# Scattering each expert's rows of a mixture-of-experts layer in two half-row transfers on separate chains

## The chip, the core and the metric

The kernel runs on one NeuronCore of a Trainium2 chip. The metric is the device time of one execution in microseconds (us). TensorE (PE, with its weight loads as PEld), VectorE (DVE), ScalarE (ACT), GpSimd (POOL) and SyncE (SP) each run their own instruction stream in order; they meet through semaphores, and 16 DMA engines move data between HBM and the on-chip memories.

## The reference, cut to what matters

```python
# x1 = x + token mixers (512 tokens, 1024 columns)
h2 = rmsnorm(x1, g_ffn)
scores = sigmoid(h2 @ w_router); top 8 of 64 experts per token -> gates (512 x 64)
for e in range(64):
    hmid = silu(h2 @ w_gate_e[e]) * (h2 @ w_up_e[e]) * gates[:, e]     # 256 wide
    routed += hmid @ w_down_e[e]                                       # 1024 wide
out = x1 + shared_swiglu(h2) + routed
```

512 tokens choose 8 experts each, so an expert has 64 tokens on average.

## The kernel before, in words

The token mixers and the router come first and take about 470 us. Then follows the expert stage, one step for each of the 64 experts, with tokens gathered 96 slots at a time (a set of 128 partition rows; the unused ones hold the index 1024 or more and are dropped by the bounds check).

For expert k a step has these parts. **SP** loads 3 MB of weights into one of four slots (`load_w`, L502). **ACT** and DVE split each weight into a high part (ACT, `gu_hi_k` L969 and `split_wd` L916) and a low part (DVE, `gu_lo_k` L1446 and `low_wd` L1457), because every product is computed as three. Both DVE lines subtract one SBUF tensor from another. **PE** makes gate and up (L1834), turns the gathered rows of the next expert (L1862), makes the down product of the expert before (L1848) in two halves of 512 columns, turns the middle (L1842) and finds the slots of a later expert (L1855). **ACT** copies each half of the down product from PSUM into `y` (`copy_y`, L934), one of two buffers. DVE works out the row indices `idxg` (L1414, four buffers), and ACT keeps a copy, `idxs` (`keep_idx`, L983), since a gather's index buffer is overwritten before the scatter is done with it.

**POOL** issues both indirect transfers. `gather` (L609) fetches the rows of expert k+5 from `hn_dram`. `scatter` (L615) adds the rows of `y` into `out` in HBM, by accumulating DMA. Before each of them POOL runs `take_turn` (L605), a tiny addition of 16 elements that reads and writes SBUF and has its own semaphore. In `scatter_k` POOL waits for both halves of `y`, for the kept indices, and for the scatter before to have landed, as two scatters may add to the same row of `out`. Around expert k the order on POOL is written out by hand:

```python
def pair(k, u):
    scatter_k(k, u, 5 + 2 * k)
    gather_k(k + 5, (u + 1) % 4, 6 + 2 * k)
```

It runs for experts 0 to 58; the last five experts have a scatter alone. Two other waits hang on a scatter's landing: ACT's `y_i` before it writes a `y` buffer again (two experts later), and `keep_idx` before it writes an index buffer again (four experts later). At the end POOL waits for the last scatter; a loop for experts with over 96 tokens follows and is entered only if there are any.

Of the kernel before, what the change touches and what calls it, by code (L numbers as in the profile page):

```python
# [31 lines left out]
P = 128  # L32
# [18 lines left out]
def layer(nc, x, g_mix, w_in, q_norm_a, k_norm_a, q_norm_b, k_norm_b, rel_bias, b_forget, w_gate, b_gate,  # L51
# [4 lines left out]
    E, D, F = w_gate_e.shape  # L56
    N = x.shape[1]
# [6 lines left out]
    COLS = 512  # L64
# [3 lines left out]
    SH = NT  # L68
# [81 lines left out]
    with ctx:  # L150
        def sb(name, shape, dt=f32):
            return ctx.enter_context(nc.sbuf_tensor(name, shape, dt))

        def sem(name):
            return ctx.enter_context(nc.semaphore(name))
# [18 lines left out]
        gsum = sb("gsum", [P, NT]); ginv = sb("ginv", [P, NT]); m8 = sb("m8", [P, NT, 8])  # L174
        gate = sb("gate", [P, 4])
        idxg = [sb(f"idxg{i}", [P, 1], u32) for i in range(4)]
        idxs = [sb(f"idxs{i}", [P, 1], u32) for i in range(4)]
        hn_ss, hn_ms, hn_r = sb("hn_ss", [P, NT]), sb("hn_ms", [P, NT]), sb("hn_r", [P, NT])
        rbias = sb("rbias", [P, E])

# [143 lines left out]
        wd_hi_ready, wd_ready, o_wd_hi, o_wd, o_midT_hi = sem("wd_hi_ready"), sem("wd_ready"), sem("o_wd_hi"), sem("o_wd"), sem("o_midT_hi")  # L324
        y_psum, y_ready = sem("y_psum"), sem("y_ready")
        based = [sem(f"based{i}") for i in range(2)]
        scattered, pool_set, turns = sem("scattered"), sem("pool_set"), sem("turns")
        o_free, o_pos, o_onehot, o_idx_psum, o_idx, o_gathered = (
            sem("o_free"), sem("o_pos"), sem("o_onehot"), sem("o_idx_psum"), sem("o_idx"), sem("o_gathered"))
        o_xT_psum, o_xT, o_gu, o_silu, o_mid, o_midT_psum, o_midT, o_y_psum, o_y, o_scattered = (  # L330
# [14 lines left out]
        def after(eng, s, n):  # L345

            if not isinstance(n, int) or n > 0:
                eng.wait_ge(s, n)
# [223 lines left out]
        def _(pool):  # L572
# [24 lines left out]
            for i in range(4):  # L597
                nc.gpsimd.memset(xg[i], 0.0).then_inc(pool_set, 1)
            pool.wait_ge(pool_set, 5)
            last_row = pool.to_reg(N - 1)  # L600

            def take_turn(before):

# [9 lines left out]
            def scatter(slot, idx, before, done):  # L613
                take_turn(before)
                pool.indirect_dma_start(out=out_rows, out_offset=bass.IndirectOffsetOnAxis(idx[:, 0:1], 0),  # L615
                                        in_=y[slot], in_offset=None, bounds_check=last_row, oob_is_err=False,
                                        compute_op=ALU.add).then_inc(done, 16)

            def gather_k(k, slot, before):
                after(pool, xT_psum, k - 3)  # L620
                pool.wait_ge(idx_ready, k + 1)
                gather(slot, before, gathered[slot])

            def scatter_k(k, u, before):
                pool.wait_ge(y_ready, 2 * (SH + k + 1))
                pool.wait_ge(idx_kept, k + 1)
                after(pool, scattered, 16 * k)
                scatter(u % 2, idxs[u], before, scattered)

            for k in range(5):  # L630
                gather_k(k, k % 4, k)
# [1 line left out]
                pool.wait_ge(b, 8 * SH)  # L633

            def pair(k, u):
                scatter_k(k, u, 5 + 2 * k)
                gather_k(k + 5, (u + 1) % 4, 6 + 2 * k)

            for k in range(4):
                pair(k, k)  # L640
# [4 lines left out]
                pair(k, k % 4)  # L645
            more = pool.value_load(rounds_i[0:1, 0:1], min_val=0, max_val=ROUNDS - 1)
            for k in range(E - 5, E):
                scatter_k(k, k % 4, 5 + 2 * (E - 5) + k - (E - 5))
            pool.wait_ge(scattered, 16 * E)

            with pool.If(more > 0):
                with pool.Fori(0, more * E) as it:
                    pool.wait_ge(o_idx, it + 1)
                    gather(0, 2 * E + 2 * it, o_gathered)
                    pool.wait_ge(o_y, it + 1)
                    scatter(0, idxg[0], 2 * E + 2 * it + 1, o_scattered)
                    pool.wait_ge(o_scattered, 16 * it + 16)
            with pool.Else():
                pass
# [2 lines left out]
        def _(act):  # L662
# [278 lines left out]
            def y_i(it, n):  # L941
                if isinstance(it, int) and it == SH:
                    for b in based:
                        act.wait_ge(b, 8 * SH)
                after(act, scattered, 16 * (it - SH - 1))
                for h in range(2):
                    act.wait_ge(y_psum, 2 * it + h + 1)
                    copy_y(n, h).then_inc(y_ready, 1)

# [29 lines left out]

            def keep_idx(k, u):  # L980
                act.wait_ge(idx_ready, k + 1)
                after(act, scattered, 16 * (k - 3))
                nc.scalar.activation(idxs[u][:], idxg[u][:], ACT.Copy).then_inc(idx_kept, 1)  # L983

            def step(it, n, slot, more=True):
                k = it - SH
# [611 lines left out]
        def _(pe):  # L1598
# [356 lines left out]

            more = pe.value_load(rounds_i[0:1, 0:1], min_val=0, max_val=ROUNDS - 1)
            with pe.If(more > 0):
                pe.wait_ge(scattered, 16 * E)
                with pe.Fori(0, more * E) as it:
                    nc.tensor.matmul(psM[0:1, 0:1], ident_b[:, 0:1], ident_b[:, 0:1], start=True, stop=True).then_inc(o_free, 1)  # L1960
                    pe.wait_ge(o_onehot, it + 1)
                    find_slots(0, it % E).then_inc(o_idx_psum, 1)
                    pe.wait_ge(o_gathered, 16 * it + 16)
                    transpose_rows(0).then_inc(o_xT_psum, 1)
                    pe.wait_ge(o_xT, it + 1)
                    for k in range(2):
                        pe.wait_ge(w_in_sem[0][k], 8 * E + 32 * it + 32)
                    gate_up(0, P, xT_all, 0).then_inc(o_gu, 1)
                    pe.wait_ge(o_mid, it + 1)
                    transpose_mid(0, P).then_inc(o_midT_psum, 1)  # L1970
                    pe.wait_ge(o_midT, it + 1)
                    pe.wait_ge(o_wd, it + 1)
                    down(0, 0, P)
                    down(0, 1, P).then_inc(o_y_psum, 1)
                    pe.wait_ge(o_y, it + 1)
# [55 lines left out]
```

## Time and profile before

| | us |
|---|---|
| median of 3 runs (lowest to highest) | 1109.51 (1108.78 to 1111.87) |
| the profiled execution, its time | 1109.88 |
| its span in the trace | 1107.9 |
| PE busy | 1082.7 (98%) |
| DVE busy | 882.5 (80%) |
| ACT busy | 738.8 (67%) |
| POOL busy | 317.4 (29%) |

All times in the rows below are microseconds from the start of the span. In a row of a timeline stand the start, the duration, the engine, the line of the kernel, the operation, output<-input with their shapes, and in square brackets how long the engine was idle before it and what ended that. Where a row stands for several instructions (x2), its duration runs from the first's start to the last's end. DVE instructions overlap by some 0.08 us at their ends. A page of the profile gives the busy time of each engine as a share of the whole span, so the expert stage has to be read by windows.

### The profile page before, as it was taken

Reading aid. Unit: us, or ns where it says so; the run is one execution under the profiler, and the core shown is the slowest. Engines: PE = TensorE matmul, PEld = TensorE weight load, DVE = VectorE, ACT = ScalarE, POOL = GpSimd, SP = SyncE. Lnnn points to the kernel's source line nnn. Section 1 sums busy time; section 2 is a strip of 40 time slices with the busy share of each in tenths; the row PEclk is TensorE's granted clock in tenths of the full one; section 3 lists DMA queues with packets and bytes.
Section 4 is the critical chain, followed back from the end, with each engine's and each line's share of the span. In section 5 each row is a group of like instructions: output and inputs, shape, how many; then the busy total and the mean of one; then the engine's idle time right before and its main releaser. Section 6 shows DMA issues by size and latency. Waiting matters only on the chain.

```text
span 1107.9 us, 19464 instructions
## 1 busy us (share of the span) xinstructions
PE 1082.7 (98%) x5809; PEld 893.6 (81%) x5809; DVE 882.5 (80%) x1405; ACT 738.8 (67%) x1304; POOL 317.4 (29%) x293
## 2 busy tenths in 40 slices
PE   8999999999999999999999999999999999999994
PEld 7789978777777887678888888888888888888883
DVE  6644376478865845579999999999999999999993
ACT  5434464444346521168888888888888888888883
POOL 1221022000000001137444444444444444434332
PEclk9999999999999999999999999999999999999998
DMA  7233212421532093669999999999999999999972
GB/s 248 78 108 106 92 41 75 152 76 39 134 114 96 7 381 138 245 231 366 382 388 384 385 376 377 376 384 386 383 375 385 377 380 377 381 380 382 378 273 36
DMA packets 97353, 284.71 MB, mean 257 GB/s; under 512 B 19683, under 2 KB 22251, under 8 KB 96924
## 3 DMA queue, kind: packets, MB, share of 16 engines
q1 hardware_dynamic: 78876, 250.52, 59.4%
q0 software_dynamic: 18432, 33.61, 12.2%
q8 instruction: 26, 0.43, 0.1%
q14 instruction: 19, 0.16, 0.0%
HBM read 279.79 MB, written 37.81 MB: 287 GB/s over the span
## 4 chain that ended last, share of the span: by engine, by line
PE 61%; DMA 24%; DVE 8%; issue 3%; ACT 2%; POOL 2%; POOLq 0%; SPq 0%; ACTq 0%; DVEq 0%
DMA out<-arena,idxs 23%; PE bank L1660 21%; PE bank L1834 17%; PE bank L1848 8%; PE bank L1808 3%; PE bank L1862 3%; PE bank L1604 2%; PE bank L1822 2%; DVE w_lo L1095 1%; POOL turn L605 1%; ACT arena L795 1%; DMA arena<-in_w_in 1%; PE bank L1842 1%; DVE gu_parts L1446 1%; PE bank L1716 1%
## 5 line engine op out<-in xcount | busy, mean ns | idle before, releaser
L1834 PE MATMUL bank<-gu_parts,xT_parts 128*128 128x512 f32 x1280 | 338.9, 394 | 0.9 <-DVE gu_parts L1446 0.5
L1834 PEld LDWEIGHTS bank<-gu_parts,xT_parts 128*128 128x128 f32 x1280 | 235.3, 188 | 47.6 <-DVE gu_parts L1446 0.9
L1848 PE MATMUL bank<-w_lo 128*128 128x512 f32 x804 | 201.6, 399 | 0.0
L605 POOL TENSOR_TENSOR turn<-minus_half 16x1 f32<-16x1 f32 x128 | 101.2, 791 | 349.5 <-DMA out<-arena,idxs 307.3
L1848 PEld LDWEIGHTS bank<-w_lo 128*128 128x128 f32 x804 | 146.3, 188 | 28.5 <-issue 0.5
L615 POOL DMA_INDIRECT out<-arena,idxs x64 | 123.4, 1927 | 19.4 <-issue 10.2
L1660 PE MATMUL bank<-w_hi,hT_hi 128*128 128x512 f32 (+1 forms) x320 | 124.4, 389 | 0.4 <-DVE w_lo L1095 0.4
L1660 PE MATMUL bank<-w_hi,hT_lo 128*128 128x512 f32 (+1 forms) x320 | 121.7, 380 | 0.0
L1660 PE MATMUL bank<-w_lo,hT_hi 128*128 128x512 f32 (+1 forms) x320 | 121.4, 380 | 0.0
L1446 DVE TENSOR_TENSOR gu_parts<-arena_x,gu_parts 128x1024 fp32r<-128x1024 f32 x96 | 116.8, 1216 | 2.4 <-ACT gu_parts L969 2.2
L1446 DVE TENSOR_TENSOR gu_parts<-arena,gu_parts 128x1024 fp32r<-128x1024 f32 x96 | 116.8, 1216 | 2.4 <-ACT gu_parts L969 2.3
L1095 DVE TENSOR_TENSOR w_lo<-arena,w_hi 128x512 fp32r<-128x512 f32 (+1 forms) x112 | 69.2, 667 | 47.3 <-ACT w_hi L694 47.3
L969 ACT ACTIVATE gu_parts<-arena_x 128x1024 fp32r<-128x1024 f32 x96 | 101.5, 1057 | 7.4 <-PE bank L1834 3.4
L969 ACT ACTIVATE gu_parts<-arena 128x1024 fp32r<-128x1024 f32 x96 | 101.5, 1057 | 5.9 <-DMA arena<-in_w_up_e 4.1
L934 ACT ACTIVATE arena<-bank 128x512 f32<-128x512 f32 x128 | 76.7, 600 | 29.3 <-PE bank L1848 27.3
L1834 PE MATMUL bank<-gu_more,xT_parts 128*128 128x512 f32 x256 | 89.3, 389 | 0.0
L609 POOL DMA_INDIRECT arena<-hn_dram,idxg x64 | 82.1, 1283 | 12.0 <-issue 6.6
L694 ACT ACTIVATE w_hi<-arena 128x512 fp32r<-128x512 f32 (+1 forms) x112 | 61.4, 605 | 29.5 <-PE bank L1660 17.1
L579 POOL TENSOR_TENSOR hn_r<-hn_ms,minus_half 128x1 f32<-128x1 f32 x8 | 4.4, 556 | 251.5 <-DVE hn_ms L1071 251.5
L1457 DVE TENSOR_TENSOR w_lo<-arena,w_lo 128x1024 fp32r<-128x1024 f32 x64 | 75.3, 1218 | 0.3 <-ACT w_lo L916 0.3
L1457 DVE TENSOR_TENSOR w_lo<-arena_x,w_lo 128x1024 fp32r<-128x1024 f32 x64 | 75.3, 1217 | 0.2 <-ACT w_lo L916 0.2
L579 POOL TENSOR_TENSOR rnorm<-mean,minus_half 128x8 f32<-128x8 f32 x20 | 32.8, 1638 | 144.7 <-DVE mean L1170 144.7
(226 smaller groups left out, 1988.6 us busy)
## 6 DMA issues: line engine op xcount, KB each, us to landing
arena<-in_w_gate_e SPq DMA_DIRECT2D x64, 512.0 KB
arena<-in_w_up_e SPq DMA_DIRECT2D x64, 512.0 KB
arena<-in_w_down_e SPq DMA_DIRECT2D x64, 512.0 KB
arena_x<-in_w_gate_e SPq DMA_DIRECT2D x64, 512.0 KB
arena_x<-in_w_up_e SPq DMA_DIRECT2D x64, 512.0 KB
arena_x<-in_w_down_e SPq DMA_DIRECT2D x64, 512.0 KB
arena<-in_w_in SPq DMA_DIRECT2D x14, 1024.0 KB, 5.5
arena<-in_w_gate SPq DMA_DIRECT2D x8, 1024.0 KB, 5.8
```

The lines of the kernel that those rows point to most:

```text
L605: nc.gpsimd.tensor_tensor(turn[:], minus_half[0:16, 0:1], minus_half[0:16, 0:1], ALU.add).then_inc(turns, 1)
L609: pool.indirect_dma_start(out=xg[slot], out_offset=None, in_=hn_dram, in_offset=bass.IndirectOffsetOnAxis(idxg[slot][:, 0:1], 0), bounds_c ...
L615: pool.indirect_dma_start(out=out_rows, out_offset=bass.IndirectOffsetOnAxis(idx[:, 0:1], 0), in_=y[slot], in_offset=None, bounds_check=la ...
L694: nc.scalar.activation(split_of(w_hi, c, j), raw_of(c, j), ACT.Copy).then_inc(split_hi, 1)
L934: return nc.scalar.activation(y[n][:, h * 512:(h + 1) * 512], psY[h][:], ACT.Copy)
L969: nc.scalar.activation(gu_hi[c].rearrange("p g j c -> p g (j c)"), wgu[slot][:, :, PER * c:PER * (c + 1), :].rearrange("p g j c -> p g (j ...
L1095: nc.vector.tensor_tensor(split_of(w_lo, c, j), raw_of(c, j), split_of(w_hi, c, j).bitcast(f32), ALU.subtract).then_inc(split_lo, 1)
L1446: nc.vector.tensor_tensor(flat(gu_lo[c]), flat(raw_part), flat(gu_hi[c]).bitcast(f32), ALU.subtract).then_inc(gu_lo_ready, 1)
L1457: return nc.vector.tensor_tensor(low[:, :, cols], wd[slot][:, :, cols], high[:, :, cols].bitcast(f32), ALU.subtract)
L1660: last = nc.tensor.matmul(psD[n % 2][:, 0:chunk_cols(c)], left, right, start=(j == 0 and k == 0), stop=(j == ND - 1 and k == 2))
L1834: last = nc.tensor.matmul(out_, a[:, PER * c + j, :], b[c][:, :, j, :], start=(c == 0 and j == 0 and i == 0), stop=(c == CHUNKS - 1 and j ...
L1848: last = nc.tensor.matmul(psY[h][0:rows, :], midT[n][a][:, j, 0:rows], w[b][:, j, h * 512:(h + 1) * 512], start=(j == 0 and k == 0), stop= ...
```

## The change

The index tile of a scatter gets two columns. ACT writes 2i and 2i+1 into them instead of i, and `out` is seen as 1024 half rows of 512 columns. An expert's scatter becomes two, one for each half of the columns of `y`, each with its own semaphore. Each half waits for its own half of `y` and for the same half of the expert before; ACT's copy of a half waits for that half alone. Each has its own turn. All 128 index rows are walked in each of the two.

```diff
-        idxs = [sb(f"idxs{i}", [P, 1], u32) for i in range(4)]
+        idxs = [sb(f"idxs{i}", [P, 2], u32) for i in range(4)]
...
-        scattered, pool_set, turns = sem("scattered"), sem("pool_set"), sem("turns")
+        scattered, pool_set, turns = [sem(f"scattered{h}") for h in range(2)], sem("pool_set"), sem("turns")
...
+            def scatter_half(h, slot, idx, before):
+                take_turn(before)
+                pool.indirect_dma_start(out=out_halves, out_offset=bass.IndirectOffsetOnAxis(idx[:, h:h + 1], 0),
+                                        in_=y[slot][:, h * COLS:(h + 1) * COLS], in_offset=None, bounds_check=last_half, oob_is_err=False,
+                                        compute_op=ALU.add).then_inc(scattered[h], 16)
...
             def scatter_k(k, u, before):
-                pool.wait_ge(y_ready, 2 * (SH + k + 1))
                 pool.wait_ge(idx_kept, k + 1)
-                after(pool, scattered, 16 * k)
-                scatter(u % 2, idxs[u], before, scattered)
+                for h in range(2):
+                    pool.wait_ge(y_ready, 2 * (SH + k) + h + 1)
+                    after(pool, scattered[h], 16 * k)
+                    scatter_half(h, u % 2, idxs[u], before + h)
...
             def pair(k, u):
-                scatter_k(k, u, 5 + 2 * k)
-                gather_k(k + 5, (u + 1) % 4, 6 + 2 * k)
+                scatter_k(k, u, 5 + 3 * k)
+                gather_k(k + 5, (u + 1) % 4, 7 + 3 * k)
...
-                after(act, scattered, 16 * (it - SH - 1))
                 for h in range(2):
+                    after(act, scattered[h], 16 * (it - SH - 1))
                     act.wait_ge(y_psum, 2 * it + h + 1)
                     copy_y(n, h).then_inc(y_ready, 1)
...
                 act.wait_ge(idx_ready, k + 1)
-                after(act, scattered, 16 * (k - 3))
-                nc.scalar.activation(idxs[u][:], idxg[u][:], ACT.Copy).then_inc(idx_kept, 1)
+                for done in scattered:
+                    after(act, done, 16 * (k - 3))
+                nc.scalar.activation(idxs[u][:, 0:1], idxg[u][:], ACT.Copy, scale=2.0)
+                nc.scalar.activation(idxs[u][:, 1:2], idxg[u][:], ACT.Copy, scale=2.0, bias=1.0).then_inc(idx_kept, 1)
```

## Rows read from the trace of the kernel before

**Rows 1.** Busy time by windows: stretch, its length, then busy us of PE, PEld, DVE, ACT, POOL, granted clock, DMA share, GB/s

```profile
600.00:700.00 100.00, 100.00 (x526) 84.64 (x525) 97.40 (x137) 87.25 (x137) 43.87 (x43) 1.00 1.03 380
...
1000.00:1050.00 50.00, 49.86 (x260) 42.01 (x260) 47.90 (x67) 43.10 (x67) 20.21 (x20) 1.00 1.03 378
```

**Rows 2.** Timeline of PE: the row transposes of two experts in succession

```profile
725.42 1.05 PE L1862 MATMUL bank<-cst,arena 128*128 128x128 f32 x8
...
734.94 1.05 PE L1862 MATMUL bank<-cst,arena 128*128 128x128 f32 x8
```

**Rows 3.** Waits over the whole span: who waited for what, us in total, times, longest

```profile
POOL turn L605 <- DMA out<-arena,idxs: 249.2, 51, 6.1
ACT xT_parts L978 <- PE bank L1862: 23.4, 50, 0.5
```

**Rows 4.** Timeline of POOL over one expert in mid-stage

```profile
726.50 0.98 POOL L605 TENSOR_TENSOR turn<-minus_half 16x1 f32<-16x1 f32 x1 [4.89 <-DMA out<-arena,idxs]
727.63 1.59 POOL L615 DMA_INDIRECT out<-arena,idxs  x1 [0.16 <-issue]
728.72 1.22 POOL L605 TENSOR_TENSOR turn<-minus_half 16x1 f32<-16x1 f32 x1
730.08 1.05 POOL L609 DMA_INDIRECT arena<-hn_dram,idxg  x1
735.97 1.02 POOL L605 TENSOR_TENSOR turn<-minus_half 16x1 f32<-16x1 f32 x1 [4.85 <-DMA out<-arena,idxs]
```

**Rows 5.** Timeline of DVE in the same stretch

```profile
721.67 2.35 DVE L1457 TENSOR_TENSOR w_lo<-arena,w_lo 128x1024 fp32r<-128x1024 f32 x2
...
726.21 1.22 DVE L1446 TENSOR_TENSOR gu_parts<-arena_x,gu_parts 128x1024 fp32r<-128x1024 f32 x1
...
728.67 1.21 DVE L1446 TENSOR_TENSOR gu_parts<-arena_x,gu_parts 128x1024 fp32r<-128x1024 f32 x1
...
731.19 1.22 DVE L1457 TENSOR_TENSOR w_lo<-arena_x,w_lo 128x1024 fp32r<-128x1024 f32 x1
```

**Rows 6.** Timeline of POOL where the expert stage begins

```profile
493.60 6.05 POOL L605 TENSOR_TENSOR turn<-minus_half 16x1 f32<-16x1 f32 x1 [5.77 <-issue]
...
502.26 1.62 POOL L615 DMA_INDIRECT out<-arena,idxs  x1 [0.16 <-POOL turn L605]
503.35 5.49 POOL L605 TENSOR_TENSOR turn<-minus_half 16x1 f32<-16x1 f32 x1
508.99 1.06 POOL L609 DMA_INDIRECT arena<-hn_dram,idxg  x1
...
512.07 7.39 POOL L615 DMA_INDIRECT out<-arena,idxs  x1 [0.52 <-DVE gate L1415]
```

**Rows 7.** Timeline of DVE beside the turn at 503.35

```profile
503.04 2.35 DVE L1457 TENSOR_TENSOR w_lo<-arena_x,w_lo 128x1024 fp32r<-128x1024 f32 x2
...
507.58 1.21 DVE L1446 TENSOR_TENSOR gu_parts<-arena,gu_parts 128x1024 fp32r<-128x1024 f32 x1
```

**Rows 8.** Timeline of POOL and DVE around 754 us

```profile
753.65 1.22 DVE L1446 TENSOR_TENSOR gu_parts<-arena_x,gu_more 128x1024 fp32r<-128x1024 f32 x1
754.28 0.63 POOL L605 TENSOR_TENSOR turn<-minus_half 16x1 f32<-16x1 f32 x1 [4.44 <-DMA out<-arena,idxs]
```

**Rows 9.** DMA queues: packets, MB, share of 16 engines, in 732.5 to 733.5, then in 728 to 732

```profile
q0 software_dynamic: 35, 0.14, 71.5%
...
q1 hardware_dynamic: 458, 1.67, 102.3%
```

**Rows 10.** Timeline of ACT: the kept indices, and the split that follows

```profile
722.35 0.20 ACT L983 ACTIVATE idxs<-idxg 128x1 uint32<-128x1 uint32 x1
722.44 1.06 ACT L969 ACTIVATE gu_parts<-arena_x 128x1024 fp32r<-128x1024 f32 x1
```

**Rows 11.** Timeline of the end: the last copy of y, the last two scatters

```profile
1094.17 1.56 POOL L615 DMA_INDIRECT out<-arena,idxs  x1 [0.46 <-issue]
1095.11 0.60 ACT L934 ACTIVATE arena<-bank 128x512 f32<-128x512 f32 x1 [0.72 <-PE bank L1848]
...
1099.62 1.56 POOL L615 DMA_INDIRECT out<-arena,idxs  x1 [0.46 <-issue]
```

**Rows 12.** Chain that ended last: start, us; the landing of the last scatter but one

```profile
1094.17 4.57 DMA out<-arena,idxs
```

More of the change, by code:

```diff
@@ L599, in _ @@
             pool.wait_ge(pool_set, 5)
-            last_row = pool.to_reg(N - 1)
+            last_row, last_half = pool.to_reg(N - 1), pool.to_reg(2 * N - 1)
+            out_halves = out_rows.rearrange("t (h c) -> (t h) c", h=2)
             def take_turn(before):
@@ L647, in _ @@
             for k in range(E - 5, E):
-                scatter_k(k, k % 4, 5 + 2 * (E - 5) + k - (E - 5))
-            pool.wait_ge(scattered, 16 * E)
+                scatter_k(k, k % 4, 5 + 3 * (E - 5) + 2 * (k - (E - 5)))
+            for h in range(2):
+                pool.wait_ge(scattered[h], 16 * E)
             with pool.If(more > 0):
@@ L653, in _ @@
                     pool.wait_ge(o_idx, it + 1)
-                    gather(0, 2 * E + 2 * it, o_gathered)
+                    gather(0, 3 * E + 2 * it, o_gathered)
                     pool.wait_ge(o_y, it + 1)
-                    scatter(0, idxg[0], 2 * E + 2 * it + 1, o_scattered)
+                    scatter(0, idxg[0], 3 * E + 2 * it + 1, o_scattered)
                     pool.wait_ge(o_scattered, 16 * it + 16)
@@ L1957, in _ @@
             with pe.If(more > 0):
-                pe.wait_ge(scattered, 16 * E)
+                for done in scattered:
+                    pe.wait_ge(done, 16 * E)
                 with pe.Fori(0, more * E) as it:
```

## The prediction

> **What bounds the kernel now.** I read the busy time by windows first, since the page's shares mix stages. In the expert stage PE is busy 100.00 of 100 us, DVE 97.4, ACT 87.3, POOL only 43.9, and the DMA engines are full (share 1.03, 380 GB/s) [rows 1]. PE turns rows every 9.52 us (725.42 to 734.94), so an expert costs 9.52 us and PE sets it [rows 2]. In 1000 to 1050 PE is still busy 49.86 of 50. Next come the waits: POOL's turn waits 249 us in all for scatters to land, 51 times [rows 3]. That looks like slack on POOL, and like a chain the change would loosen. Neither holds without a look at when POOL can work, so the third view is POOL's timeline beside DVE's.
>
> There a pattern shows. DVE's splits (L1446, L1457) read two SBUF tensors. POOL's turn takes 0.98 us at 726.50 and ends 0.05 after the split that ends at 727.43; the next takes 1.22 us, at 728.72, and ends 0.06 after the one that ends at 729.88 [rows 4, 5]. An addition of 16 elements needs no such time: it is shut out. So POOL works in two windows per expert: 727.43 to 728.67 (1.24 us), where scatter is issued, and 729.88 to 731.19 (1.31), where gather is. From 731.19 on five splits follow without a gap, two of L1457 and three of L1446 (the same five stand from 721.67 to 727.43: 5.76 us) [rows 5]. One job, turn and issue, uses 727.43 to 728.72, 1.29 us, in the first window, and 729.88 to 731.13, 1.25, in the second [rows 4]. Both windows are full: 2.54 of 2.55 us. The 4.9 us that POOL waits for landings lie inside the closed block, where it couldn't have worked in any case.
>
> That a job which comes too late pays for the whole block can be read where the stage begins: a turn of 6.05 us at 493.60, one of 5.49 at 503.35, an issue of 7.39 at 512.07 [rows 6]. The turn at 503.35 began just as L1457 did (503.04) and ended at 508.84, 0.05 behind the last L1446 (507.58 + 1.21) [rows 7].
>
> **The change, part by part.**
>
> *POOL's third job.* Each of experts 0 to 58 now has three jobs (two halves and a gather), each with its turn, in place of two. All 128 index rows are walked in each, so I price a half's job like a whole one's, 1.25 us of open time. The low bound is half of that by bytes: then three jobs need 2.5 us, fit, and the term is 0; but the walk is over rows, and gather, a plain transfer of the same 128 rows, takes as long as scatter does. Three jobs need 3.75 us of open time and DVE's pattern has 2.55. Since gathers and scatters must keep pace with experts, DVE has to stand still until the rest fits: 3.75 - 2.55 = 1.20 us per expert at least. How it comes to stand: POOL falls behind, ACT's copy of y (a buffer written again two experts later) waits for a half to land, the middle's copy and the down split queue behind that copy on ACT, and DVE has nothing to do between its single split and the next L1457. POOL's second window opens wider there. PE then waits for the down split and the middle. The upper bound: the opening comes when a landing is late, not when POOL asks; a turn that just misses pays one more split of 1.21 us, so 2.41. Farther out, a third job that always pays for the whole block gives three windows per expert, one and a half DVE patterns: 14.28 us, 4.76 more. I take 1.60: the 1.20, and 0.4 for turns that miss, since a turn falls into a split at any point and then waits half of it, 0.6 us, and two of three jobs can meet one (2/3 x 0.6 = 0.4). Experts that pay: 59, less 2 that the second y buffer and the gathers ahead cover: 57. Term: 57 x 1.60 = +91 us; bounds 57 x 1.20 = +68 and 57 x 2.41 = +137.
>
> *ACT's second index copy.* An index copy takes ACT from 722.35 to 722.44, 0.09 us until the next starts [rows 10]; once more per expert. Hidden: ACT waits 0.5 us for the row transposes in each of 50 experts [rows 3]. Without that cover, 64 x 0.09 = 6 us. Taken as 0. ACT's and keep_idx's further waits for a second semaphore cost nothing where the first is waited for already.
>
> *The packets.* Bytes stay. In the stretch with only accumulating packets on the software queue 35 of them hold 71.5% of 16 engines for 1 us: 0.327 us each; a plain one costs 1.023 x 4 x 16 / 458 = 0.143 [rows 9]. A half row's packet may cost 0.164 (by bytes) or 0.327 (by packet). The added DMA time per expert lies between 0 and 64 x 0.327 / 16 = 1.3 us. As the cost of a whole one is 2.3 times a plain one's, as two passes over the bytes would give, I take it by bytes, near 0. In my case even 1.3 would be hidden: a step of 11.1 us leaves the engines 1.6 more.
>
> *The waits between halves.* Behind POOL's wait for the first half's landing stand the second half and the gather. A scatter was issued at 727.63 and had landed by 735.97 [rows 4]; with its two chains each half has a whole step for that, so these waits end before the windows open, as now. Priced 0.
>
> *The end.* The last five experts have two jobs, as before, so no stretch. The last scatter is issued at 1099.62 although y was ready at 1095.71; it waited for the one before, 4.57 us from issue to landing [rows 11, 12]. After: the first half of expert 62 at 1092.4, the second 2.2 later, landing in 3.9 to 4.57, then the last half by 1099.1 to 1099.9, landed at 1103.0 to 1104.5, where now it is 1099.62 + 4.57 = 1104.2. Term: -1 us (-1.2 to +0.3).
>
> Sum against the profiled execution's own time: 1109.9 + 91 - 1 = 1200 us (its span is 1107.9, 2.0 less; its time lies 0.4 above the median of 1109.51, too little to correct).
>
> A rule is to be weighed against this. POOL's turn at 503.35 met four borders between splits and was let in at none of them [rows 6, 7]; the one at 754.28 was let in at the first border, 754.91 (753.65 + 1.22 is 754.87) [rows 8]. The Trainium skill (SBUF — State Buffer, section on the two separate sides) says that DVE with two SBUF inputs and a GpSimd operation that reads SBUF exclude each other, whoever is first, for the whole instruction. By that rule as it stands each border would let POOL in, and the third job would pay some 1.2 us of waiting inside a block of 5.76 and nothing on the path. The row at 503.35 speaks against it, that at 754.28 for it. Without the rule the case stands as a rival:
>
> **The rivals.**
>
> *POOL gets in between splits.* If turns like that at 754.28 are the rule, three jobs, each 1.25 plus at most 1.22 of waiting, fit in 9.52 (7.4 us). Then the body stays at 9.52 us per expert, and the packets go by bytes. The end gives its -1: 1109 us, 1107 to 1113. For it: the turn at 754.28. Against: that was a turn, while the issue at 512.07 stayed shut out for 7.39 us [rows 6], and one job per window is all that POOL does.
>
> *The body holds and the end is shorter*, the faster case. If POOL has room, scatters may also follow their data more closely; the last half would be issued as soon as the last y is there, 1095.71 + 0.6, and land 4.57 later: 1100.9 in place of 1104.2, 3.3 less, and up to 1 more if a half lands sooner. 1105.5 us. It decides from the point where the second half of expert 62 lands before 1096, which needs its issue by 1091.5, a us ahead of its data: hard.
>
> *DMA becomes the bound.* POOL has room, but an accumulating half packet costs what a whole one does: 1.3 us per expert over 58 experts is +75, and -1 at the end: 1184 us. For it: the engines are full, and nothing shows a shorter accumulating packet. Against: plain packets here go by bytes.
>
> *The whole block each time*: 57 x 4.76 = +271: 1381 us.
>
> **How the numbers follow.** Forecast 0.66; POOL gets in 0.13; shorter end 0.08; DMA 0.09; whole block 0.04. A measurement of this kernel can tell about 0.3% (3.3 us) from no change. Faster: 0.08. Same: 0.11 of the 0.13. Slower: 0.66 + 0.09 + 0.04 + 0.02 = 0.81. The likeliest case's own range is 1177 to 1246; openings that come still later, as far as one more split for a second job (57 x 0.6 = 34 on average), draw it up to 1280, and a lighter half job down to the case of no change. To hold 8 in 10 the low end must reach into the case of no change: 1108 to 1280.
>
> **What would show it.** Right: PE transposes 10.7 to 12 us apart in mid-stage, often in two alternating lengths; turns or issues on POOL of 5 to 7 us beside unbroken splits in each step or each second; ACT's copy of y waiting for the scatter's DMA; the DMA share under 1. Wrong: steps of 9.52, with turns of about 1 us inside the block (then POOL gets in), or a DMA share of 1 with ACT waiting for weights (then the packets). A half's issue well under 1 us would break the first term.

## The result, and the profile after

The changed kernel takes 1117.3 us (median of 4 runs, 1114.12 to 1119.11) where the kernel before, on the same chip, takes 1109.17: a ratio of 1.0071, 95% interval 1.0056 to 1.0086. It is slower, by 0.7%. The profiled execution took 1117.17 us, its span is 1115.4. Of the 83 us that the forecast stood too high, nearly all lies in one term.

Busy time by windows of the changed kernel, in the columns of [rows 1], shows where the time isn't and where it is:

```profile
600.00:700.00 100.00, 100.00 (x526) 84.63 (x525) 97.41 (x136) 88.20 (x146) 78.07 (x63) 1.00 1.04 381
900.00:1000.00 100.00, 98.88 (x506) 82.29 (x505) 92.89 (x131) 83.31 (x142) 74.53 (x63) 1.00 1.04 375
```

In mid-stage PE is as busy as in [rows 1]; POOL's share has gone from 43.87 to 78.07 us of 100 and nobody waits for it. From 900 on PE has gaps; the count of its matmuls shows more than the busy time does, 506 in 100 us where it was 526. The row transposes of PE (its timeline, [rows 2]) date the loss. The changed kernel:

```profile
906.98 1.05 PE L1873 MATMUL bank<-cst,arena 128*128 128x128 f32 x8
916.77 1.05 PE L1873 MATMUL bank<-cst,arena 128*128 128x128 f32 x8
...
946.56 1.05 PE L1873 MATMUL bank<-cst,arena 128*128 128x128 f32 x8
956.80 1.05 PE L1873 MATMUL bank<-cst,arena 128*128 128x128 f32 x8
...
1085.30 1.05 PE L1873 MATMUL bank<-cst,arena 128*128 128x128 f32 x8
```

The kernel before:

```profile
1011.41 1.05 PE L1862 MATMUL bank<-cst,arena 128*128 128x128 f32 x8
1021.25 1.05 PE L1862 MATMUL bank<-cst,arena 128*128 128x128 f32 x8
...
1078.37 1.05 PE L1862 MATMUL bank<-cst,arena 128*128 128x128 f32 x8
```

From 506 to 906.98 the steps are 9.52 to 9.57 us in both, as in [rows 2], and the two kernels are some 0.4 us apart. Then the changed kernel's become 9.79, later 10.24 at 956.80, and the last transposes come 6.93 us later than before (1085.30 against 1078.37). The kernel before has the same break, later and milder, at 1021.25 (9.84). What PE misses there is named by the waits between 900 and 1080 us (who waited for what, us in total, times, longest); the changed kernel:

```profile
DVE gu_parts L1457 <- ACT gu_parts L978: 12.9, 18, 1.4
...
ACT gu_parts L978 <- DMA arena<-in_w_up_e: 10.4, 8, 1.8
ACT gu_parts L978 <- DMA arena_x<-in_w_up_e: 9.1, 6, 2.0
```

In the kernel before the first of the two DMA rows reads (the second: 2.1 us, 3 times, 0.8):

```profile
ACT gu_parts L969 <- DMA arena<-in_w_up_e: 4.1, 5, 1.1
```

Weights come late. The DMA queues say why (packets, MB, share of 16 engines, 600 to 900 us). Before:

```profile
q1 hardware_dynamic: 26640, 97.00, 81.2%
q0 software_dynamic: 9178, 17.08, 22.0%
```

After:

```profile
q1 hardware_dynamic: 26545, 96.66, 80.7%
q0 software_dynamic: 13762, 17.14, 23.8%
```

The software queue (gathers and scatters) moves the same bytes in half as many packets again and takes 1.8% of 300 us more: 5.4 us of all 16 engines over 31.5 experts, 0.17 us per expert. Where no short packets mix in, one accumulated packet of the software queue takes 0.327 us for a whole row [rows 9] and 0.176 for a half (66.0% of 16 engines for 0.5 us, over 30 packets; changed kernel, 725.5 to 726):

```profile
q0 software_dynamic: 30, 0.06, 66.0%
```

Two halves so cost 8% more than one whole. The lead of the loads can be read at SP, which issues them: it waits until DVE has read the slot that the next load will overwrite, and as long as it waits, the loads are ahead. SP's waits from 800 to 900 us, kernel before, then changed kernel:

```profile
SPq L502 <- DVE w_lo L1457: 25.8, 10, 4.9
```

```profile
SPq L502 <- DVE w_lo L1468: 8.9, 6, 3.2
```

(SPq is SP's queue; the columns are those of the waits above.) From 700 to 800 they are 61.0 and 48.4 us, from 900 to 1000 they are 0.8 and nothing. How long the lead lasts also differs between runs: tail_halves, below, which is the kernel before up to the last expert, still has 32.1 us from 900 to 1000. In these two profiles the lead is gone earlier in the changed kernel, and its steps break some eleven experts earlier. From there each step lasts as long as its transfers take: 9.93 us on average from 906.98 to 1055.93, where PE would need 9.53. That is more than the added 0.17, since the whole excess shows once the lead is gone; the kernel before has 9.65 in its few late steps (1011.41 to 1059.68).

What the prediction thought impossible stands in POOL's timeline of the changed kernel (start, duration; compare [rows 4]):

```profile
601.76 0.98 POOL L606 TENSOR_TENSOR turn<-minus_half 16x1 f32<-16x1 f32 x1 [1.53 <-DMA out<-arena,idxs]
602.90 2.39 POOL L622 DMA_INDIRECT out<-arena,idxs  x1 [0.16 <-issue]
604.76 0.60 POOL L606 TENSOR_TENSOR turn<-minus_half 16x1 f32<-16x1 f32 x1
605.60 2.13 POOL L622 DMA_INDIRECT out<-arena,idxs  x1 [0.24 <-issue]
607.19 0.60 POOL L606 TENSOR_TENSOR turn<-minus_half 16x1 f32<-16x1 f32 x1
608.03 1.73 POOL L610 DMA_INDIRECT arena<-hn_dram,idxg  x1 [0.24 <-issue]
611.19 1.08 POOL L606 TENSOR_TENSOR turn<-minus_half 16x1 f32<-16x1 f32 x1 [1.44 <-DMA out<-arena,idxs]
```

Beside it the splits in DVE's timeline, same kernel:

```profile
602.61 1.21 DVE L1457 TENSOR_TENSOR gu_parts<-arena_x,gu_parts 128x1024 fp32r<-128x1024 f32 x1
...
607.60 2.35 DVE L1468 TENSOR_TENSOR w_lo<-arena,w_lo 128x1024 fp32r<-128x1024 f32 x2
609.87 1.22 DVE L1457 TENSOR_TENSOR gu_parts<-arena_x,gu_parts 128x1024 fp32r<-128x1024 f32 x1
611.01 1.22 DVE L1457 TENSOR_TENSOR gu_parts<-arena_x,gu_more 128x1024 fp32r<-128x1024 f32 x1
```

The five-split block begins at 607.60, and gather is issued at 608.03, inside it. The first scatter's issue at 602.90 lies beside the split at 602.61 too. Issues are not shut out there; they only last longer, 1.73 to 2.39 us where they take 1.05 to 1.59 in [rows 4]. (One issue on record stands against this, the 7.39 us in [rows 6]; more_bytes and before_less, below, have it at the same place, 7.42 and 7.39 us, and the kernels with three jobs don't. It stays unexplained.) The turn at 611.19 begins inside the block and is let in at the border at 612.23 (611.01 + 1.22), with the block's last split still to come. From the first turn to the end of gather's issue three jobs take 8.0 us (601.76 to 609.76) of 9.53.

The kernel before had shown the same already. One hundred us ahead of the expert in [rows 4] its POOL and its DVE read:

```profile
631.51 2.06 POOL L615 DMA_INDIRECT out<-arena,idxs  x1 [0.50 <-PE bank L1862]
633.87 1.60 POOL L609 DMA_INDIRECT arena<-hn_dram,idxg  x1 [0.24 <-issue]
```

```profile
633.34 1.22 DVE L1446 TENSOR_TENSOR gu_parts<-arena,gu_parts 128x1024 fp32r<-128x1024 f32 x1
```

Gather's issue begins inside a split. Of the 42 scatters issued from 600 to 1000 us 23 last 1.6 us as in [rows 4] and 19 last 2.0 to 2.4. Even in [rows 4] the issue at 727.63 runs to 729.22, past the split's start at 728.67 [rows 5].

At the end of the span, the timelines of ACT and POOL in the changed kernel, to be set beside [rows 11]:

```profile
1101.86 0.60 ACT L943 ACTIVATE arena<-bank 128x512 f32<-128x512 f32 x1 [0.78 <-PE bank L1859]
1103.66 0.18 POOL L606 TENSOR_TENSOR turn<-minus_half 16x1 f32<-16x1 f32 x1 [0.38 <-DMA out<-arena,idxs]
1104.31 1.56 POOL L622 DMA_INDIRECT out<-arena,idxs  x1 [0.47 <-POOL turn L606]
...
1106.83 1.56 POOL L622 DMA_INDIRECT out<-arena,idxs  x1 [0.90 <-issue]
```

From the end of the last copy of y (1102.46) to the end of the span are 12.9 us; before, 1107.9 - 1095.71 = 12.2. The end costs 0.7 us more; with the 6.93 of the steps (some 0.4 of it from before the stage's steps) that is the difference of the spans, 7.5, within 0.2.

### The profile page after: what moved, and what is told of

Same layout as the page of the kernel before. It is cut to its first block, busy times and chain, and to the rows that moved or that the text cites. A ratio compares the mean times of both kernels' runs of the same rounds, so it can differ in the third digit from the quotient of the medians.

```text
span 1115.4 us, 19794 instructions
## 1 busy us (share of the span) xinstructions
PE 1087.5 (98%) x5809; PEld 895.1 (80%) x5809; DVE 882.0 (79%) x1405; ACT 742.0 (67%) x1368; POOL 497.7 (45%) x421
## 4 chain that ended last, share of the span: by engine, by line
PE 76%; DVE 8%; SPq 7%; DMA 3%; ACT 2%; issue 2%; POOL 1%; ACTq 0%; DVEq 0%; POOLq 0%
PE bank L1845 26%; PE bank L1671 21%; PE bank L1859 13%; SPq L502 7%; PE bank L1873 4%; PE bank L1819 3%; PE bank L1615 3%; PE bank L1833 2%; DMA arena<-in_w_up_e 2%; DVE w_lo L1106 1%; PE bank L1853 1%; DVE gu_parts L1457 1%; ACT arena L804 1%; PE bank L1727 1%; PE bank L1740 1%
## 5 line engine op out<-in xcount | busy, mean ns | idle before, releaser
L622 POOL DMA_INDIRECT out<-arena,idxs x128 | 262.6, 2051 | 31.5 <-issue 26.0
L606 POOL TENSOR_TENSOR turn<-minus_half 16x1 f32<-16x1 f32 x192 | 161.0, 839 | 163.1 <-DMA out<-arena,idxs 88.8
L978 ACT ACTIVATE gu_parts<-arena 128x1024 fp32r<-128x1024 f32 x96 | 101.4, 1057 | 11.3 <-DMA arena<-in_w_up_e 10.4
L610 POOL DMA_INDIRECT arena<-hn_dram,idxg x64 | 94.3, 1473 | 12.9 <-issue 11.8
```

Of the source, the lines that this page charges most:

```text
L606: nc.gpsimd.tensor_tensor(turn[:], minus_half[0:16, 0:1], minus_half[0:16, 0:1], ALU.add).then_inc(turns, 1)
L610: pool.indirect_dma_start(out=xg[slot], out_offset=None, in_=hn_dram, in_offset=bass.IndirectOffsetOnAxis(idxg[slot][:, 0:1], 0), bounds_c ...
L622: pool.indirect_dma_start(out=out_halves, out_offset=bass.IndirectOffsetOnAxis(idx[:, h:h + 1], 0), in_=y[slot][:, h * COLS:(h + 1) * COLS ...
L978: nc.scalar.activation(gu_hi[c].rearrange("p g j c -> p g (j c)"), wgu[slot][:, :, PER * c:PER * (c + 1), :].rearrange("p g j c -> p g (j ...
```

## The experiments

Three theories were to be told apart: that POOL's room between DVE's splits is the price (the forecast, theory P), that it is time on the full DMA engines (theory D), and that the two chains matter in themselves.

**DMA engines with room.** The kernel before and the changed one, each with the same part of the loads of w_down_e left out from expert 8 on (three quarters of the columns of the second half of the rows, 0.39 MB per expert):

```diff
-                    sp.dma_start(dst[:, i * rows:(i + 1) * rows], src[:, i * rows:(i + 1) * rows]).then_inc(w_in_sem[n][k], 16)
+                    cols = D // 4 if short and i else D if k == 2 else F
+                    sp.dma_start(dst[:, i * rows:(i + 1) * rows, 0:cols], src[:, i * rows:(i + 1) * rows, 0:cols]).then_inc(w_in_sem[n][k], 16)
...
-                    load_w(n, 2, k)
+                    load_w(n, 2, k, short=True)
```

> The kernel before, with the second half of w_down_e loaded for 256 of its 1024 columns from expert 8 on, so 0.39 MB less per expert (the down weights used are then partly stale). Theory D (DMA engines full: half packets cost more engine time, weights come late in the last third): the kernel before loses only about 1 us to late weights (steps of 9.84 and 9.74 near the end), so 1107 to 1109 us. Theory P (POOL's third job) says nothing on this one: same as before.

> The changed kernel with the same 0.39 MB less per expert. Theory D: the loss goes; steps of 9.53 us to the end, 1108 to 1110 us, within 2 us of the relieved kernel before, the rest being a slightly longer end. Theory P (the third job on POOL and the second index copy on ACT delay the step): the 7 to 8 us stay, 1115 to 1117 us, as neither depends on the loads.

Measured: 1108.1 us (ratio 0.9983, 0.9974 to 0.9992) and 1109.59 (0.9999, 0.9989 to 1.0008). Busy time by windows of the changed kernel with fewer bytes, columns as above:

```profile
900.00:1000.00 100.00, 100.00 (x526) 84.65 (x525) 97.30 (x138) 88.81 (x148) 71.56 (x65) 1.00 1.03 345
```

SP's waits from 800 to 900 us, the gauge of the lead, in the same kernel:

```profile
SPq L503 <- DVE w_lo L1469: 60.9, 10, 6.4
```

PE has no gap left in the stretch where it had lost 1.12 us, and POOL does its three jobs all the same. The DMA share alone would not have shown the room: it reads 1.03 here too, at 345 GB/s in place of 375. So some 6.5 of 8 us went with the bytes, and were time of the DMA engines; 1.5 us stay by the medians, 1.9 by the spans (1107.3 against 1105.4). The last transposes stand at 1077.17 and 1077.04, 0.13 apart, so what stays lies behind them: the last issue is at 1098.80, and at 1097.27 without the halves.

**The same price paid by other packets.** Into the kernel before I put a plain load of 32 KB per expert, 128 packets of 256 B (more_bytes):

```diff
+            def load_spare(n, e):
+                src = w_down_e[bass.ds(e, 1)].rearrange("o (p j) f -> p (o j) f", p=P)
+                sp.dma_start(spare[n][:], src[:, 0, 0:64]).then_inc(spare_in[n], 16)
```

> The kernel before with one more load per expert from SP, 32 KB as 128 packets of 256 bytes into a spare tile: by the packet times of the trace (0.018 us each) 0.15 us of all 16 engines per expert, near the 0.17 that the change adds. POOL, ACT and DVE do nothing more. Theory D: steps grow in the last third as in the changed kernel, 1114 to 1118 us. Theory P: no change, 1109 us.

and a third job of POOL with next to no bytes, a turn and a gather of 4 B per row (small_third):

```diff
+            def tiny_k(k, u, before):
+                after(pool, tiny_in, 16 * k)
+                take_turn(before)
+                pool.indirect_dma_start(out=tiny[:], out_offset=None, in_=hn_dram.rearrange("t (c o) -> (t c) o", o=1),
+                                        in_offset=bass.IndirectOffsetOnAxis(idxs[u][:, 0:1], 0),
+                                        bounds_check=last_row, oob_is_err=False).then_inc(tiny_in, 16)
```

> The kernel before with a third job on POOL for experts 0 to 58, its turn included: an indirect gather of 4 bytes for each index row. POOL is as busy as in the changed kernel, but the packets are 0.009 us each, 0.08 us of the engines per expert. Theory D: 57 x 0.08 = 5 us of engine time, of which the lead takes some: 1110 to 1114 us. Theory P: all of the loss, 1116 to 1118 us.

Measured: 1115.44 us (1.0048, 1.0032 to 1.0064) and 1114.54 (1.0035, 1.0025 to 1.0046). Both keep steps of 9.51 to 9.57 until 897 and then have steps of up to 10.60 and 10.12, 9.86 and 9.71 on average. The plain load never touches POOL, so a loss of this shape needs no third job; it cost 5.5 us where the change cost 8.1, each against the kernel before in the same set of runs. The third job with next to no bytes cost 4.6 us, which the packets' time does not explain in size. From 600 to 900 us both queues together hold 103.2% in the kernel before, 103.5 with the small third job, 103.7 with the plain load and 104.5 in the changed kernel: the order is that of the losses, but they are not in proportion. In small_third the software queue holds 22.3% in place of 22.0, 0.03 us per expert, while SP's waits from 800 to 900 us are down to 5.9 us, as in the changed kernel. What a third transfer takes from the loads beyond the time of its packets stays open.

**Turns alone** (turns): two turns ahead of every job of POOL in the kernel before, no packet added.

```diff
-                after(pool, turns, before)
-                nc.gpsimd.tensor_tensor(turn[:], minus_half[0:16, 0:1], minus_half[0:16, 0:1], ALU.add).then_inc(turns, 1)
+                for i in range(2):
+                    after(pool, turns, 2 * before + i)
+                    nc.gpsimd.tensor_tensor(turn[:], minus_half[0:16, 0:1], minus_half[0:16, 0:1], ALU.add).then_inc(turns, 1)
```

> The kernel before with two turns ahead of each of GpSimd's indirect transfers, so GpSimd must get in twice more per expert, with no added packet. Theory (a visit of GpSimd that fits between VectorE's splits costs nothing): 1109 to 1111 us, all transposes 9.53 us apart until about 1011 us. Rival (the small part of the loss that the added bytes do not explain comes from VectorE being held at the added visits): 1112 us or more, with steps of 9.6 us and above from 550 us on.

Measured: 1112.58 us, ratio 1.0025 (1.0009 to 1.0042), 12 runs spread from 1108.19 to 1117.3. The profiled one (1108.68) has each step as before. Neither theory's number: the median is the rival's, the steps are the theory's. In a spread of 9 us one profile of a quick run can't say what the longer ones do. What two more turns cost stays open; the two turns are let in together (timeline of POOL):

```profile
735.91 1.05 POOL L606 TENSOR_TENSOR turn<-minus_half 16x1 f32<-16x1 f32 x2 [4.82 <-DMA out<-arena,idxs]
```

**Where POOL's room ends.** Four quarters on four chains, five jobs per expert (quarters), its double with fewer weight bytes (quarters_less, the same part of w_down_e left out), and half plus two quarters, four jobs, also with fewer bytes (three_pieces_less):

```diff
-                for h in range(2):
-                    pool.wait_ge(y_ready, 2 * (SH + k) + h + 1)
+                for h in range(4):
+                    pool.wait_ge(y_ready, 2 * (SH + k) + h // 2 + 1)
                     after(pool, scattered[h], 16 * k)
                     scatter_half(h, u % 2, idxs[u], before + h)
```

> The change carried one step further: four transfers of 256 columns on four chains, so five jobs on POOL per expert. Theory D, from packets of 0.327 us for a whole accumulated row and 0.177 for a half: 0.027 + 0.075 per KB, so 0.102 for a quarter and 256 x 0.102 - 64 x 0.327 = 5.2, with some 2.5 for the dropped rows and completions, 0.48 us of all engines per expert, some 25 us in all: 1131 to 1138 us, if POOL has room for five jobs. If POOL's open time bounds at five jobs (5 x 1.25 = 6.25 us of open time, where DVE leaves 2.55), the steps are 10.5 us or more from the first experts on, over 1150 us.

> The same with 0.39 MB of w_down_e less per expert (stale down weights), 0.94 us less of all engines. Theory D: the DMA engines have room, so what is left is POOL's: steps of 9.53 us and 1109 to 1112 us if five jobs fit; over 1140 us if POOL's open time bounds.

> The changed kernel with the second half of the columns sent as two quarters: four jobs of GpSimd per expert (three scatters and a gather), on three chains, and with part of the w_down_e loads left out from expert 8 on, so that the DMA engines have room. Theory (GpSimd's jobs fit as long as their sum, each with its share of shut-out time, stays below a step of 9.53 us: three take 8.3 us of it, from the first turn to the end of the gather's issue, a fourth 2.1 to 2.4 us more): steps of 10.4 to 10.7 us, that is 1155 to 1178 us. Rival (what slowed the four-quarter kernel was its many small packets or its five index columns, not GpSimd's room): 1110 to 1114 us, steps 9.53 us.

Measured: quarters 1219.72 us (1.0984, 1.0968 to 1.1), with fewer bytes 1228.22 (1.1027, 1.0998 to 1.1056), three pieces 1125.27 (1.0166, 1.0129 to 1.0202). Windows of quarters, and the waits of the y copy in 600 to 1000 us:

```profile
600.00:700.00 100.00, 91.05 (x436) 74.01 (x435) 81.97 (x116) 74.65 (x143) 90.24 (x89) 0.95 1.01 329
```

```profile
ACT arena L943 <- DMA out<-arena,idxs: 83.6, 35, 4.4
DVE w_lo L1465 <- ACT w_lo L940: 64.6, 25, 4.1
```

and windows of the three pieces:

```profile
600.00:700.00 100.00, 99.74 (x524) 84.22 (x523) 96.64 (x138) 88.68 (x157) 90.07 (x83) 1.00 1.03 340
```

With five jobs the picture that I had forecast for three is there to the letter: steps of 9.5 to 10 us between others of 11 to 15, the y copy waiting for a landing, DVE idle ahead of its down split behind that copy. Fewer bytes don't help, so DMA is not its bound. With four jobs most steps are still 9.53 us, with POOL 90% busy; there are three large ones (11.42 us up to 527.30, 14.30 up to 551.24, 14.10 up to 863.26) and a few of 9.6 to 10.3. My expectation of 10.4 to 10.7 in every step failed: back to back, four jobs need 9.59 us from turn to turn (in POOL's timeline from 609.25 to 618.84), since the long first turn and the wait for a landing shrink when POOL has no time to spare. That is a little over a step. So POOL's room is just short of four jobs, not two.

**Larger packets**, an attempt to buy back engine time: each weight load as one transfer of 1 MB in place of two (merged, from the kernel before; after_merged, from the changed one).

```diff
-                for i in range(2):
-                    sp.dma_start(dst[:, i * rows:(i + 1) * rows], src[:, i * rows:(i + 1) * rows]).then_inc(w_in_sem[n][k], 16)
+                sp.dma_start(dst, src).then_inc(w_in_sem[n][k], 16)
```

> The kernel before with each weight load as one transfer of 1 MB in place of two of 512 KB, so 128 packets of 8 KB in place of 256 of 4 KB (0.309 us each in the trace in place of 2 x 0.159) and half the completions: some 0.25 us less of all engines per expert. Theory D: what late weights cost goes, as in the relieved kernel: 1107 to 1109 us, ratio 0.998.

> The changed kernel with the same merged loads. Theory D: the 0.25 us saved cover the 0.17 added: 1108.5 to 1111 us, so the change costs about 1 us in place of 8, with the whole computation done. Theory P: 1115 to 1117 us.

Both missed: 1120.05 us (1.0099, 1.0075 to 1.0123) and 1130.63 (1.0167, 1.0145 to 1.0188). Theory D had its own part right: the rate rose a little (queue q1 holds 80.4% for 32.98 MB in 600 to 700 us, against 81.9% for 32.47 before), and in merged SP waits 81 us from 900 to 1000, so the loads keep their lead. But single steps jump to 10.3 to 10.9. Waits of merged in 880 to 1060 us, then POOL's and DVE's timelines at such a jump:

```profile
POOL turn L603 <- DMA out<-arena,idxs: 89.0, 18, 7.2
ACT arena L932 <- DMA out<-arena,idxs: 11.0, 11, 2.0
```

```profile
946.73 5.83 POOL L603 TENSOR_TENSOR turn<-minus_half 16x1 f32<-16x1 f32 x1
952.71 1.04 POOL L607 DMA_INDIRECT arena<-hn_dram,idxg  x1
```

```profile
946.76 2.35 DVE L1455 TENSOR_TENSOR w_lo<-arena,w_lo 128x1024 fp32r<-128x1024 f32 x2
...
951.30 1.21 DVE L1444 TENSOR_TENSOR gu_parts<-arena_x,gu_parts 128x1024 fp32r<-128x1024 f32 x1
```

The y copy now waits for a scatter to land, which it doesn't in the kernel before, and a turn that starts with the first split of the block (946.73 and 946.76) is shut out over all five splits and ends 0.05 us after them (952.56; 951.30 + 1.21 = 952.51). I read it so: beside packets twice as long the scatter's packets land later, and POOL falls out of the places where it fits. That the landing is what packet length changes was argued from these waits and not measured by itself. The Trainium skill (DMA: Bandwidth & Descriptors, section on bandwidth) asks for transfers of at least 1 MiB; in this kernel, with a small latency-bound queue beside the loads, that loses 1%.

**What the chains are worth.** Both halves wait for both halves of y and for both transfers of the expert before (one_chain); then each of the two edits alone (chain_only, y_together):

```diff
-                    pool.wait_ge(y_ready, 2 * (SH + k) + h + 1)
-                    after(pool, scattered[h], 16 * k)
+                    pool.wait_ge(y_ready, 2 * (SH + k) + 2)
+                    for done in scattered:
+                        after(pool, done, 16 * k)
```

> The changed kernel, but each half waits for both halves of y and for both halves of the expert before, so the two transfers still leave separately while the two chains are tied into one. Theory (the loss is the engine time of the added packets, and the chains buy nothing): 1115 to 1119 us, as the changed kernel, with transposes 9.53 us apart until about 907 us. Rival (the separate chains had hidden part of a larger cost, by letting the first half leave early and spreading the traffic): slower than the changed kernel by more than 3 us, steps above 9.53 us earlier.

> The changed kernel with one edit: each half waits for both halves of the expert before to land, not for its own alone; the first half still leaves as soon as its half of y is there. Theory (the time from a scatter's issue to its landing is some 8 us of a step of 9.53, so on one chain the second issue, 1.9 us later, makes the loop 10.6 us, and only two chains keep it below a step): 1180 to 1225 us, as with both waits tied, and GpSimd's turn waits for the landing in every expert. Rival (the loss came from holding the first half back until the second half of y is there): 1115 to 1120 us, as the changed kernel.

> The changed kernel with the other edit: the first half waits until both halves of y are there, and the two chains stay separate. Theory (the chains carry the effect, and the early leave of the first half, some 1 to 2 us, is slack): 1115 to 1120 us. Rival (the early leave is what keeps the first chain in time): 1180 to 1225 us.

Measured: one_chain 1202.43 us (1.0741, 1.0687 to 1.0795), chain_only 1191.88 (5 runs), y_together 1116.58 (1.0063, 1.0046 to 1.008). The five runs of chain_only lie far apart, 1169.98 to 1203.04 us, that is 5.4 to 8.4% above the kernel before; its quickest and the quickest of one_chain (1180.35) are still 50 us and more above the changed kernel. My theory for the first, that the chains buy nothing, fell by 85 us; the rival's held. The chain of work in one_chain, 600 to 640 us (start, us, what):

```profile
604.84 0.47 POOL out L622
...
606.74 7.88 DMA out<-arena,idxs
...
614.85 0.18 POOL turn L606
...
616.54 0.60 POOL turn L606
617.39 7.19 DMA out<-arena,idxs
```

A loop closes through the landing: turn and first issue, then the second issue 1.90 us later (604.84 to 606.74), 7.88 until it has landed, the next turn at 614.85, the next first issue at 615.49: 10.65 us, where a step may take 9.53. Steps from 600 us on are 9.5 to 14.4. In chain_only the loop is as long (first issues at 644.10 and 654.91, 10.81 us apart). In the kernel before the same loop has one issue: 727.63 to 735.97 to 737.15 in [rows 4], 9.52 us, just one step, in which the turn still waits out a split. Two chains give each half such a loop of its own. y_together shows that the early leave of the first half is worth nothing.

**The end alone** (tail_halves): only the last expert's result in halves, in the kernel before.

```diff
+            k = E - 1
+            pool.wait_ge(idx_kept, k + 1)
+            after(pool, scattered, 16 * k)
+            for h, done in enumerate((scattered, scattered_hi)):
+                pool.wait_ge(y_ready, 2 * (SH + k) + h + 1)
+                scatter_half(h, (k % 4) % 2, idxs[k % 4], 2 * E - 1 + h, done)
```

> The kernel before with only the last expert's result scattered in two halves. Theory (at the end a second issue stands behind the first, and the transfer's own time is hardly shorter): the stretch from the last y copy to the end of the span 12.2 to 13.5 us, where it is 12.2 in the kernel before; time 1109 to 1111 us. Rival (as the prediction had it, the last transfer carries half the bytes and lands earlier): that stretch 11.2 us, time 1108 to 1109 us.

Measured: 1109.92 us (1.0007, 0.9998 to 1.0016). POOL's timeline:

```profile
1099.85 1.56 POOL L623 DMA_INDIRECT out<-arena,idxs  x1 [0.47 <-POOL turn L607]
1100.88 0.60 POOL L607 TENSOR_TENSOR turn<-minus_half 16x1 f32<-16x1 f32 x1
1101.72 1.56 POOL L623 DMA_INDIRECT out<-arena,idxs  x1 [0.24 <-issue]
```

The span ends at 1109.5, 7.8 us behind the second issue; before, it ends 8.3 behind the only one (1099.62). Half the bytes save 0.5 us, and the second issue comes 1.87 after the first. From the last y copy (ended 1096.43) to the end are 13.1 us, within the theory's range.

## Why the prediction was wrong

- **What bounds the kernel now** was half read. PE sets the step, right. But the same row shows the DMA engines at a share of 1.03, and the step at 1021.25 and the late waits for w_up_e, which the prediction doesn't name, show that the loads' lead is spent by then. SP's waits, 61.0 us from 700 to 800 and 0.8 from 900 to 1000, had the lead running out in the kernel before; a share of 1.03 alone did not say so. The waits of [rows 3] are those of 500 to 1000 us, not of the whole span (there 307.3 us, 63 times).
- **POOL's third job**, +91 us with the bounds +68 to +137: this is the step that failed. It priced turn and issue together as work that needs a stretch without a split. Only the turn does, at times; the issue runs beside splits, 1.7 to 2.4 us long in the changed kernel. Three jobs take 8.0 of 9.53 us, no step grows, and the term is 0. The error had its place in [rows 4]: the turn at 735.97 lay inside the block because the landing released it there, and I took its end at a border as evidence of a closed block. One expert was read as the pattern of all, though 19 of 42 scatters in mid-stage had the longer issue. The closed block was seen only in [rows 6], from the start of the stage. The changed kernel has turns of this kind too, of 6.04, 5.49 and 5.49 us; all of 5 us and above lie before 520.
- **The rule that was weighed.** The Trainium skill (SBUF — State Buffer, section on who interferes with whom) has a splitting DVE instruction with two SBUF inputs block a GpSimd instruction that reads SBUF, not one that only writes it. For the addition the trace agrees in the main: at 611.19 it waits for the border. The issue reads its index column from SBUF too, yet it is stretched (1.73 to 2.39 us) and not held for whole splits. The case in which POOL gets in at borders, 1109 us by the prediction, was the nearer one. The rule does not explain every row: turns of 5.36 to 6.05 us pass over the borders of a block in every kernel here (6.3 where there are two in one), and one issue lasts 7.39 us.
- **The mechanism of the forecast** (y copy waits for a landing, DVE idles ahead of the down split, alternating steps) is real, and came with the fifth job: 1219.72 us.
- **The packets**, priced by bytes near 0, bounds 0 to 1.3 us per expert: the bounds held, the choice was too low. 0.17 us per expert was measured. The cover that I named (a step of 11.1 us) went with the first term, and the case that had POOL get in priced the packets at nothing. By the software queue's share 0.17 over 57 experts is 9.7 us; 6.9 is what the last transposes moved. This term carries the result, though small_third leaves open how much of it is the packets' length and how much a further transfer. The plain packet was priced a little low as well: the 458 packets of [rows 9] average 3.6 KB, so a full one of 4 KB takes 0.159 us (a half-us window without short packets, 744.5 to 745), and a whole accumulated one 2.1 times that, not 2.3.
- **The waits between halves**, 0, for the reason given, that with its own chain each half has a whole step. Right, and chain_only puts the price of tied chains at 5 to 8% of the changed kernel.
- **ACT's second index copy**, 0: nothing in the trace speaks against it (in after_less PE has no gap); it was not tried alone.
- **The end**, -1 us (-1.2 to +0.3): it is +0.7, and between the two kernels with fewer bytes 1.8 (span less last transposes: 30.13 against 28.36). The last scatter waits for the one before, as was said, but then a second issue stands ahead of it, and a half lands hardly sooner (0.5 us in tail_halves).
- **The rivals.** "POOL gets in between splits" (1109 us, chance 0.13) had the mechanism and missed the packets; "DMA becomes the bound" (1184, 0.09) had the resource and a price over seven times too high (1.3 against 0.17). The result is their mixture. It lies in the range of 1108 to 1280, whose low end was there for the first of them.

## What to carry to other kernels

Before an engine's odd waits are made into a forecast, ask which of its instructions is shut out and by what, and take the evidence from the stage where the change acts, not from the stage's first steps. Look too at how the waits of the load-issuing engine change along the stage: while it waits for a free slot the loads are ahead, and where the waits fade the lead is running out, which a busy share doesn't show. Where the loads have no time to spare, splitting a transfer costs engine time even at equal bytes (0.17 us per expert here), and it shows only when the lead is gone. And if a transfer that must land before its successor leaves is split, give each part a semaphore of its own: the loop of issue and landing (9.5 us with one issue in it, 10.7 to 10.8 with two) must fit into the step.

## What was not expected of the hardware

- An addition on POOL of 16 elements takes 0.18 us free, 0.60 right behind an issue, about 1.0 to 1.25 where it waits for a border, and 5.36 to 6.05 where it is shut out over a block of five (6.3 for a pair, in turns). The last happened in all kernels at the stage's start (DVE busy without a gap), and in mid-stage in merged, after_merged and one_chain, and once each in quarters (537.84, 5.54 us) and three_pieces_less (826.09, 5.55 us). The ones set beside DVE's timeline begin within 0.5 us of the start of the block's first split, before or behind it. That alone doesn't decide: in after_merged the turn at 646.01, 0.25 us behind such a start (645.76), takes 5.55 us, and the one at 763.50, also 0.25 behind (763.25), takes 1.01. What decides stays open.
- With gaps in PE's work the mean granted clock falls below the upper of its two levels, 1.2 and 2.4 GHz: 0.95 with PE busy 91.05 of 100 us (quarters, 600 to 700) and 0.98 with 92.97 (chain_only, 900 to 1000), where it is 1.00 with 98.45 (chain_only, 700 to 800). A part of those losses is the clock's.
- Larger packets on one queue made the kernel slower (1.0099), with the other queue's landings waited for; that the landings are the way was argued, not shown.
